# Gates as two float16 parts instead of three bfloat16 parts in a one-core layer stack

## What is computed

```python
def block(xb):
    q = (xb @ w_query).reshape(PEER_TOKEN_BLOCK, PEER_HEADS, 2, D_KEY // 2)
    s = jnp.einsum('thpc,pkc->thpk', q, sub_keys)
    s1, i1 = lax.top_k(s[:, :, 0], PEER_TOPK)
    s2, i2 = lax.top_k(s[:, :, 1], PEER_TOPK)
    ...
    sc, ci = lax.top_k(cand, PEER_TOPK)
    e = take(i1, ci // PEER_TOPK) * N_KEYS + take(i2, ci % PEER_TOPK)
    g = jax.nn.softmax(sc, axis=-1)
    act = jax.nn.gelu(jnp.einsum('td,thkd->thk', xb, expert_u[e]))
    return jnp.einsum('thk,thkd->td', g * act, expert_v[e])
```

## Time and profile before

| | |
|---|---|
| median of 3 runs | 1254.07 us |
| lowest and highest run | 1253.68 and 1257.48 us |
| span of the profiled execution | 1253.4 us |
| PE busy | 1233.4 us, 98% |
| weight loads | 1179.2 us, 94% |
| DVE busy | 748.6 us, 60% |
| ACT busy | 707.5 us, 56% |
| POOL busy | 649.4 us, 52% |

### The profile page before, as it was taken

How to read it: one execution, slowest core, us unless ns; L and a number is a source line. 1 busy time by engine, 2 the same in 40 slices (tenths; PEclk the granted TensorE clock), 3 DMA queues, 4 the chain that set the end, 5 groups by cost and what they waited for, 6 DMA issues and landing times.

```text
span 1253.4 us, 27356 instructions
## 1 busy us (share of the span) xinstructions
PE 1233.4 (98%) x10165; PEld 1179.2 (94%) x10165; DVE 748.6 (60%) x1501; ACT 707.5 (56%) x1276; POOL 649.4 (52%) x285
## 2 busy tenths in 40 slices
PE   8999999999999999999999999999999999999997
PEld 6888999999999999999999999999999988899886
DVE  3553069980288889995666666565557742356323
ACT  5585444444687777775545454545564655446554
POOL 7757868888876666661000000000047766677655
PEclk9999999999999999999999999999999999999999
DMA  6735545656544444446566555555665443454442
GB/s 241 263 105 199 187 146 189 196 189 200 188 154 150 150 152 152 153 152 210 193 193 192 193 193 195 191 197 188 199 238 186 135 134 120 135 201 145 139 137 101
DMA packets 59704, 218.76 MB, mean 175 GB/s; under 512 B 6720, under 2 KB 7016, under 8 KB 59248
## 3 DMA queue, kind: packets, MB, share of 16 engines
q1 hardware_dynamic: 57024, 206.14, 50.3%
q0 software_dynamic: 1760, 8.89, 1.9%
q10 hardware_dynamic: 848, 2.75, 0.5%
HBM read 215.50 MB, written 4.21 MB: 175 GB/s over the span
## 4 chain that ended last, share of the span: by engine, by line
PE 95%; ACT 1%; DVE 1%; DMA 1%; POOL 1%; issue 1%; DVEq 0%; SPq 0%
PE W L516 28%; PE A L516 28%; PE A L540 4%; PE A L560 4%; PE A L541 4%; PE A L545 4%; PE A L567 4%; PE A L562 4%; PE W L795 3%; PE A L693 1%; PE A L688 1%; PE A L690 1%; PE W L976 1%; POOL ringl L449 1%; DMA PICKT<-H 1%; PE W L947 1%
## 5 line engine op out<-in xcount | busy, mean ns | idle before, releaser
L449 POOL TENSOR_TENSOR ringl<-ring,ringh 128x1024 fp32r<-128x1024 f32 x137 | 337.8, 2484 | 147.7 <-ACT ringh L1046 127.9
L479 POOL TENSOR_TENSOR ringl<-ring,ringh 128x1024 fp32r<-128x1024 f32 x126 | 302.2, 2398 | 96.3 <-ACT ringh L1217 64.9
L516 PE MATMUL W<-XTh,ringh 128*128 128x256 f32 x1024 | 289.4, 283 | 0.1
L516 PE MATMUL W<-XTl,ringh 128*128 128x256 f32 x1024 | 283.9, 277 | 0.0
L516 PE MATMUL W<-XTh,ringl 128*128 128x256 f32 x1024 | 283.8, 277 | 0.0
L516 PE MATMUL A<-Hh,ringh 128*128 128x256 f32 x1024 | 282.8, 276 | 0.0
L516 PE MATMUL A<-Hl,ringh 128*128 128x256 f32 x1024 | 282.6, 276 | 0.0
L516 PE MATMUL A<-Hh,ringl 128*128 128x256 f32 x1024 | 282.6, 276 | 0.0
L1046 ACT ACTIVATE ringh<-ring 128x1024 fp32r<-128x1024 f32 x135 | 141.8, 1057 | 141.1 <-PE A L545 47.0
L1217 ACT ACTIVATE ringh<-ring 128x1024 fp32r<-128x1024 f32 x189 | 197.6, 1046 | 0.0
L516 PEld LDWEIGHTS W<-XTh,ringl 128*128 128x128 f32 x1024 | 193.2, 189 | 0.0
(11 more groups left out here) (272 smaller groups left out, 2057.2 us busy)
## 6 DMA issues: line engine op xcount, KB each, us to landing
ring<-exp_u SPq DMA_DIRECT2D x128, 512.0 KB, 3.3
ring<-exp_v SPq DMA_DIRECT2D x128, 512.0 KB, 4.2
ring<-w SPq DMA_DIRECT2D x72, 512.0 KB, 3.3
ring<-w_out SPq DMA_DIRECT2D x24, 512.0 KB, 3.3
ring<-w_in SPq DMA_DIRECT2D x20, 512.0 KB, 3.7
ring<-w_query SPq DMA_DIRECT2D x16, 512.0 KB, 3.6
skewed<-scratch POOLq DMA_DIRECT2D x1, 2048.0 KB, 12.0
H<-lng POOLq DMA_DIRECT2D x2, 1024.0 KB, 7.3
```

The source lines that it names most:

```text
L449: pool.tensor_tensor(ringl[:, slot, :], ring[:, slot, :], ringh[:, slot, :].bitcast(F32), ALU.subtract)\
L479: pool.tensor_tensor(ringl[:, slot, :], ring[:, slot, :], ringh[:, slot, :].bitcast(F32), ALU.subtract)\
L516: last = pe.matmul(dst, stationary[a], moving[b], start=start and n == 0, stop=stop and n == 2, skip_group_check=True)
```

## The change

The gates are carried as two float16 parts of gate x 2^14 instead of three bfloat16 parts of the gate. Both parts and both hot matrices become float16. The first part is the gate times 2^14, rounded; the second is what is left of it. The factor is taken out where the gates are applied: in DVE's `apply_gates`, which becomes a scalar_tensor_tensor (gates x 2^-14 x h), and in ACT's `copy_gates`, with the scale of the copy. PE's loop at L794 runs over `GATE_PARTS` and so issues 8 matmuls a quad.

```diff
-BF16 = mybir.dt.bfloat16
+F16 = mybir.dt.float16
...
-GATE_PARTS = 3
+GATE_PARTS = 2
+GATE_SCALE = 2.0 ** 14
...
-        GP = sb("GP", [P, GATE_PARTS, T], BF16)
+        GP = sb("GP", [P, GATE_PARTS, T], F16)
...
-        halves = X[:, :, :].rearrange("p b d -> p (b d)").bitcast(BF16)
+        halves = X[:, :, :].rearrange("p b d -> p (b d)").bitcast(F16)
         FIRST_HOT = halves[:, 0:2 * 4 * P].rearrange("p (s n e) -> p s n e", s=2, n=4)
-        GATED_HOT = halves[:, 2 * 4 * P:4 * 4 * P * 2].rearrange("p (s n a e) -> p s n a e", s=2, n=4, a=GATE_PARTS)
+        GATED_HOT = halves[:, 2 * 4 * P:2 * 4 * P * (1 + GATE_PARTS)].rearrange("p (s n a e) -> p s n a e", s=2, n=4, a=GATE_PARTS)
...
                 act.activation(H[:, c:NK, 4 * quad:4 * quad + 4],
                                W4[:, quad % 2, :].rearrange("p (t e) -> p e t", t=4)[:, c:NK, :],
-                               ACT.Copy).then_inc(gate_act, 1)
+                               ACT.Copy, scale=1.0 / GATE_SCALE).then_inc(gate_act, 1)
...
             for a in range(GATE_PARTS):
-                step(dve.tensor_copy(GP[:, a, :], A8[:, 2, :]))
+                scale = 1.0 if a else GATE_SCALE
+                step(dve.tensor_scalar(GP[:, a, :], A8[:, 2, :], scale, None, ALU.mult))
                 if a + 1 < GATE_PARTS:
-                    step(dve.tensor_tensor(A8[:, 2, :], A8[:, 2, :], GP[:, a, :], ALU.subtract))
+                    step(dve.scalar_tensor_tensor(out=A8[:, 2, :], in0=A8[:, 2, :], scalar=scale, in1=GP[:, a, :],
+                                                  op0=ALU.mult, op1=ALU.subtract))
...
                 h = H[:, 0:c, 4 * quad:4 * quad + 4]
-                dve.tensor_tensor(h, W4[:, quad % 2, :].rearrange("p (t e) -> p e t", t=4)[:, 0:c, :], h, ALU.mult)\
-                    .then_inc(gate_dve, 1)
+                dve.scalar_tensor_tensor(out=h, in0=W4[:, quad % 2, :].rearrange("p (t e) -> p e t", t=4)[:, 0:c, :],
+                                         scalar=1.0 / GATE_SCALE, in1=h, op0=ALU.mult, op1=ALU.mult).then_inc(gate_dve, 1)
```

## The result

The changed kernel takes 1239.32 us in the median of 4 runs (1237.12 to 1240.61) against 1255.7 us for the kernel before (4 runs, 1253.68 to 1257.48; the fourth, at 1257.34, came on top of the three whose median of 1254.07 the prediction used): a ratio of 0.9871, 95% interval 0.9854 to 0.9888. The profiled execution after took 1240.61 us with a span of 1238.8; in all four runs the time is 1.8 us above the span.

What follows compares the result with a forecast made beforehand. PE was taken to set the stage's pitch, DVE close behind. 62 quads x 0.223 us = 13.8 us off the span of 1253.4, plus 0.7 to the runs' median, gave 1240.2 us, range 1236.8 to 1243.6.

Steps and rivals of the forecast that it cites:

- the sign: Whole kernel: faster by over 0.3% (below 1250.3 us), chance 0.95.
- Step 1: PE's gate matmuls at L795: 8 instead of 12 a quad at 55.8 ns each, saving 0.223 us a quad.
- Rival C: Gate matmuls at L795: float16 priced like float32, 112 ns each, 14 us slower, 1268 us; chance 0.03.
- Rival A: The stage's units change their own pace: all fast 1237.5 us, all slow 1243.1; chance 0.25 for either or part.
- Step 2: End of the stage, ahead of L810: the last two quads' 0.45 us gains nothing, PE waits; 62 quads count, 13.8 us.
- Step 4: DVE's gated hot columns: 609 to 477 ns each, 0.52 us less a quad, hidden behind PE and priced at nothing.
- Step 5: DVE's apply_gates as a scalar_tensor_tensor with an immediate: no cost, no gain; upper bound twice the time an element.
- rival B: DVE becomes the bound late in the stage if apply takes twice the time an element: about 1241.5 us; chance 0.05.
- The sum's frame: Whole kernel: profiled span 1253.4 - 13.8 = 1239.6 us, plus 0.7 for the runs' median above that span.

Runs made afterwards that it cites:

- bf16_two: The changed kernel with both parts and both hot matrices in bfloat16 instead of float16: 1240.71 us (4 runs), stage 202.99 us.
- f16_one: The changed kernel with one float16 part, so 4 gate matmuls a quad: 1249.4 us (1 run), stage 192.38 us, 30 units slow.
- sixteen: The kernel before with a fourth gate matmul rereading the first part, so 16 a quad: 1278.8 us (1 run), stage 230.93 us, no slow units.
- f16_three: The changed kernel with three float16 parts, so 12 gate matmuls a quad: 1255.34 us (10 runs), ratio 1.0005, stage 219.85 us.
- dve_two: The kernel before with two bfloat16 parts made by DVE but still 12 gate matmuls a quad: 1254.3 us (10 runs), ratio 1.0001, stage 219.85 us.
- bank_swap: The kernel before with the PSUM banks of even and odd quads' gates exchanged: 1257.0 us (1 run), stage 219.84 us, slow units in the same order.
- tail_split: The changed kernel with the last but one unit's column finished behind the last quad's apply: 1250.87 us (median of 9 runs), stage 202.92 us.
- pe_two: The kernel before, DVE still making three bfloat16 parts but PE multiplying only two (8 gate matmuls a quad): 1258.18 us (10 runs), ratio 1.0009.
- tail_turn: tail_split with four idle 128-column matmuls added ahead of the down products: 1251.18, 1239.6, 1251.55 and 1259.4 us.
- late_down: The changed kernel with PE also waiting for the last finished column of H ahead of the down products: 1242.55 us (4 runs).

## Why the prediction was right, and where not

The time (1240.2 forecast, 1239.32 measured) and the sign were right, but the nearness of the two numbers is partly luck. Against the profiled run of 1240.61 the sum is 1240.2 - 2.9 (the units' pace) + 1.1 (how a span stands to its time) + 2.3 (lost elsewhere in that execution) = 1240.7: three errors that nearly cancel. Between the medians the gain is 16.4 us where 13.8 was forecast; the base of 1254.07 was a median of three that a fourth run moved to 1255.7. The low end of the range is 0.3 too low by the prediction's own terms (1239.8 - 2.7 = 1237.1, not 1236.8), which changes nothing here.

1. **Step 1, the gates' matmuls: right.** 256 fewer at 55.8 ns is 14.3 us. The chain's pieces fell from 0.69 to 0.46 us, 0.23 a quad against 0.223, and a weight load with a 128-column float16 matmul costs what the bfloat16 one costs (bf16_two, 0.01 us apart over the stage). Rival C is gone. The 81 ns for such a pair that the Trainium skill gives ("TensorE: Matmul & The Clock Gate", section "Back-to-back issue gap") would by estimate (256 x 81) have made the stage 20.7 us shorter from this term alone; at 55.8 it is 14.3, and the whole stage became 16.85 shorter.

2. **Rival A came true, in the fast direction.** All units take 2.79 us: 30 x 0.09 = 2.7 to 2.9 us more than the forecast. With it the stage's sum closes: 14.3 + 2.9 - 0.43 for the longer pause = 16.8, measured 16.85. The prediction gave A 0.25 and said a stream of 8 might leave another phase than one of 12; f16_one and sixteen show that the length of the gates' stream decides as long as PE does not pause, and f16_three, bf16_two, dve_two and bank_swap that number type, DVE's load and PSUM bank do not. The step that failed is the weight: the prediction had seen that the unit behind the stream of 24 was fast, the one row that tied the pace to the number of matmuls, and did not use it for a stream of 8.

3. **Step 2, the end of the stage: the size right, the reason half.** The pause grew by 0.43 us where 0.45 was foretold. The chain from the last but one unit by ACT's ring conversion is right. But it goes on through POOL, not through ACT's copy and DVE's last column: DVE's split of column 0 took 736 ns in the changed kernel because POOL's subtraction ran until 550.86, and tail_split, which cleared the copy and the column, made the stage only 0.08 us shorter. With the 421 ns that it takes beside an idle POOL the split would have ended at 550.82, not 551.14: 0.32 of the pause of 0.60 us. The split on DVE is a tensor_tensor with two SBUF inputs, and the kernel before has the same: its first split took 511 ns and ended at 568.06, 0.28 us after POOL's subtraction.

4. **Step 4, DVE's hot columns: the size right, the price right only together.** 475 ns against 477 foretold. "Hidden" is what dve_two shows (ratio 1.0001). But the word undersells it: without this part, with 8 matmuls on PE, DVE sets a cycle of 3.52 us and 6.1 of the stage's 16.85 us are lost (pe_two). The 13.1 us of slow down products came in that run too, but that DVE's load causes them is not shown: tail_turn has them with two parts on DVE. The prediction said that DVE's cycle was 3.54 without a pause at the end and would fall to 3.02; what it did not write is that a third of the stage's gain depends on it.

5. **Step 5 and rival B: nothing, as taken.** The apply is 556 ns in the mean before and after. B's ground was misread, though. All four executions of L1762 in the kernel before (duration ns min/median/max):

```profile
L1762 DVE SCALAR_TENSOR_TENSOR H<-H x4: 1758/3210/3917, 984.1 to 1151.6; 128x1536 f32<-128x1536 f32 x4
```

The shortest is 1758 ns for 1536 columns of two float32 SBUF sources, 1.14 ns each; it is the mean, 3024, that looked like twice the time an element. The long ones are waits for POOL, as the same trace shows. One of them, and POOL's subtraction beside it:

```profile
987.06 3.92 DVE L1762 SCALAR_TENSOR_TENSOR H<-H 128x1536 f32<-128x1536 f32 x1
```

```profile
985.48 3.88 POOL L449 TENSOR_TENSOR ringl<-ring,ringh 128x1024 fp32r<-128x1024 f32 x1
```

POOL's ends at 989.36 and DVE's at 990.98, 1.62 us later. The other two long ones (3040 and 3379 ns) end 1.61 us behind a subtraction of POOL's that was under way when they started. The short one started with POOL idle, and there POOL's subtraction, begun 0.92 us later, took 3.10 us in place of 2.40. The Trainium skill's rule ("Vector Engine (DVE) Microarchitecture Reference", section "Points that are easy to get wrong") of half throughput for such sources is not borne out by these rows: the time behind the wait is 1.61 or 1.62 us each time, one nanosecond a column.

6. **The sum's frame: off by two small things.** A run's time lies 1.8 us above its own span, not 0.7 as the comparison with a median suggested, so the forecast should have been set 1.1 higher. And the profiled span after is only 14.6 us shorter where the stage is 16.85: 2.3 us are lost elsewhere in that execution. They are in one place in the second layer, where PE waits for a small transfer (the chain, first before, then after):

```profile
1100.62 7.32 DMA PICKT<-H
...
1108.08 1.16 PE W L922 x16
```

```profile
1083.11 8.64 DMA PICKT<-H
...
1091.88 1.98 PE W L923 x16
```

The transfer took 1.3 us more, and behind it the granted clock was at its lower level (1.2 GHz) for 3.4 us (the columns of the earlier trace rows):

```profile
1092.00:1095.40 3.40, 3.40 (x23) 3.18 (x24) 0.35 (x1) 1.97 (x3) 2.36 (x1) 0.50 0.03 11
```

From ACT's piece ahead of the transfer to the next sixteen matmuls of L923 that is 17.59 us (1082.69 to 1100.28) against 14.69 before (1100.21 to 1114.90), 2.9 us more; the rest of the execution gave 0.6 back. bf16_two, with the same stage, has no such dip, 15.16 us there and a span of 1236.1. So this is the spread of executions rather than a cost of the change.

## What to carry to other kernels

Before pricing a saving on the bounding engine, take the cycle of the next engine without its pauses and ask whether the same change shortens that one too; here DVE's half alone brought nothing, PE's half alone 10.8 us of the stage, and both together 16.85, which is 1.3% of the kernel. Two instructions that do not touch the same data can still hold each other up: where one engine's short instruction is suddenly long in one place, look at what the neighbour runs at that moment. And judge a change of less than 1% on a stage's length in the trace, which repeated to 0.01 us here, while runs of one kernel can lie 7 or 13 us apart.

## What the runs showed that I had not expected

- **A stream of float32r products has two paces at one granted clock.** 113.4 ns (1512 matmuls in 171.65 us) or 118.0 (178.35), 334.79 or 347.88 us for 2952, both at clock 1.00. In these long streams the pace stayed the same until something else came between. In the stage it depends on the number of gate matmuls in between while PE does not pause, as above; with pauses of 0.1 to 0.3 us it changed behind 8 as well (pe_two). In the first 66 units it changes from run to run (slow in four traces of fourteen), and at the entry of the down products from kernel to kernel and run to run: slow in the traces of pe_two, f16_one, sixteen and tail_turn, fast in the others. A pause of 1.42 us did not bring it (late_down), four short matmuls did not cure it (tail_turn). What sets it there stays open, and so does whether the changed kernel's 1257.24 is such a run. It is worth up to 20 us in this kernel, more than the change.
- **A DVE instruction with two SBUF inputs waits for POOL's subtraction under way.** The split of 256 columns: 421 ns alone, 736 and 1745 beside it, ending 0.28 us after POOL's instruction each time. L1762, 1536 columns: 1758 ns alone, up to 3917 beside it, ending 1.61 or 1.62 us after POOL's. DVE's hot columns, with one input in PSUM, kept their length beside POOL: 604 to 618 ns over all 256.
- **The granted clock fell behind some waits of PE and not behind others.** It was 0.50 for 3.4 us after PE had waited 2.9 us for DVE in pe_two, and again for 3.4 us at the wait of 3.3 us for the small transfer in the trace after. In f16_one PE waited 2.9 us for the same transfer, and the clock stayed at 1.00. What decides is not shown.
